# A weight ring of four whole blocks, low parts written over the raw weights, and two row buffers for the gathers of UP, in a decoder block with an expert layer (one core)

## The chip, the core and the metric

The kernel runs on one core of one Trainium2 chip. The metric is the device time of one execution in microseconds; lower is better. The names of the engines in the profile are PE (TensorE), DVE (VectorE), ACT (ScalarE), POOL (GpSimd) and SP (SyncE, which here only issues transfers); PEld is TensorE's weight load.

## What is computed

A decoder block on 256 tokens of width 2048: a mixer (differential attention beside a causal convolution, a shared output projection, norms and gates from a conditioning vector), and then an expert layer, which takes about three quarters of the time and is what the change touches:

```python
q = (h @ w_q).reshape(T, PEER_HEADS, PEER_KEY_DIM)
...
    v1, i1 = lax.top_k(s1, PEER_TOPK)
    v2, i2 = lax.top_k(s2, PEER_TOPK)
...
    top, pos = lax.top_k(cand, PEER_TOPK)
    idx = jnp.take_along_axis(cand_idx, pos, axis=-1)
    g = jax.nn.softmax(top.astype(jnp.float32), axis=-1)
    u = u_tab[idx]
    vv = v_tab[idx]
    act = jax.nn.gelu(jnp.einsum('thkd,td->thk', u, hb).astype(jnp.float32),
                      approximate=False) * g
    return jnp.einsum('thk,thkd->td', act.astype(vv.dtype), vv)
```

There are 16384 experts, each one row of 2048 floats in `u_tab` and one in `v_tab` (128 MB each), and every token picks 16 of them in each of 8 heads.

## The kernel before

**Two ways through the tables.** For 192 of the 256 tokens the kernel computes the products with all experts, and so streams both tables through SBUF in 128 blocks of 1 MB each. For the other 64 tokens it gathers the chosen rows: 64 gathers of 128 rows (1 MB) from `u_rows`, later 64 from `peer_v`, issued by GpSimd (L518).

**Units and phases.** A block is worked on as two units of 128x1024 floats. All weights from the query projection on pass through the same pipeline in five phases: WQ (32 units), UP (64), MID (64), ROUTE (128), all of these with stationary weights from the ring, and DOWN (256 units, the second table). All phases from UP on are loops with 16 units (8 blocks) in one iteration: 4 of UP, 4 of MID, 8 of ROUTE, 16 of DOWN. In the profile WQ runs from 482 us, UP from 586, MID from 745, ROUTE from 934 and DOWN from 1299 to 1964 us.

**What one unit passes through.** SP loads it into one of four places of `raw` (`ring`, 512 KB each). ACT makes its high part, `w_hi` (L720, a rounding copy to the faster matmul format), DVE its low part, `w_lo` = raw - `w_hi` (L379). PE multiplies with `w_hi` (L996 in the products of UP, MID and ROUTE, L1345 in DOWN), then with `w_lo` (L1005, L1345). `w_hi` and `w_lo` have two places each. So ACT's `hi` of unit s waits for its landing, for PE to be through with `w_hi` of unit s-2 (`hi_used`), and for the low part of s-2; the low part of s waits for its high part and for PE to be through with `w_lo` of s-2 (`split_used`); and SP loads unit s when the low part of unit s-4 is made (`slot_free`). `hi_ready`, `lo_ready` and `landed` count what is made and landed.

**What else DVE does between the low parts**, in the order in which the code has it, with no way round for a later instruction: in UP and MID two chains of top-k steps per iteration (`experts`); in MID and ROUTE the dots of gathered rows with the tokens (`dots_at`, L1422, two halves for a row, at the unit numbers in `DOTS_MID`, `DOTS_ROUTE` and their `_FIRST` forms for a phase's first iteration); in ROUTE six sets of masks (`make_masks`, L1387 and L1392); in DOWN half a row per two units added up (`add_row`, L1849) and two groups of gates multiplied and split (L1814, L1821, L1823), whose inputs SP brings back from DRAM (`gel_group`, L423).

**Row buffers.** The rows of `u_rows` land in three buffers (`got[0:3]`), so gather n waits until row n-3 is used (`row_used`). Those of `peer_v` land in four.

**At the end** SP brings back the saved residual (`x_saved`, 2 MB) and ACT, at the start of DOWN, the gate row (`gate_saved`, 1 MB).

## Time and profile before

| | |
|---|---|
| median of 3 runs | 1988.01 us (1985.76 to 1992.11) |
| the profiled execution | 1988.32 us, its span 1986.4 us |
| PE, DVE busy | 92%, 81% |
| ACT, POOL busy | 42%, 8% |
| transfers | 618.02 MB, mean 311 GB/s |

The span is from the first to the last instruction; some 2 us of the execution lie outside it. A share of busy time is an average over stages that differ much, so the stretches of time below are cut at the phases and at whole iterations of their loops. "DMA share" is the mean busy share of the 16 DMA engines.

### The profile page before, as it was taken

The numbers are of one execution on the slowest core, as the hardware profiler recorded it, in microseconds if no ns is written. First come the engines' busy times: TensorE is split into PE (matmuls) and PEld (weight loads), VectorE is DVE, ScalarE is ACT, GpSimd is POOL, SyncE is SP. The second block draws the span as 40 slices with busy tenths as digits, with TensorE's granted clock in tenths as the row PEclk, the third lists the DMA queues.
The fourth block names the chain that finished last, engine by engine and source line by source line (L and its number), as shares of the span: only waits on it lengthen the run. The fifth ranks groups of instructions, "written<-read, shape, count | busy, mean of one in ns | idle before, by whom it ended". The sixth has DMA issues, their size and how long they took to land.

```text
span 1986.4 us, 30520 instructions
## 1 busy us (share of the span) xinstructions
PE 1831.6 (92%) x9902; PEld 1559.0 (78%) x9902; DVE 1611.1 (81%) x2621; ACT 843.9 (42%) x1208; POOL 160.3 (8%) x145
## 2 busy tenths in 40 slices
PE   4999999997999998888899999989999999999997
PEld 4888887435999997778899999976767777777775
DVE  4668898575878999999899999968777777777777
ACT  3011222203545554445455555544444444444444
POOL 0000000000000001000112111111101111011100
PEclk9999999998999999999999999999999999999999
DMA  8997565797886778878899999989998989989895
GB/s 349 417 422 302 218 243 218 320 394 280 302 332 194 235 240 312 284 266 276 302 354 350 357 347 359 350 326 338 320 331 314 337 318 331 330 302 334 321 322 197
DMA packets 135955, 618.02 MB, mean 311 GB/s; under 512 B 16049, under 2 KB 24785, under 8 KB 99025
## 3 DMA queue, kind: packets, MB, share of 16 engines
q1 hardware_dynamic: 105984, 464.57, 63.5%
q0 software_dynamic: 18496, 134.24, 18.9%
q10 hardware_dynamic: 11410, 18.36, 2.5%
q8 instruction: 38, 0.62, 0.1%
q14 instruction: 27, 0.22, 0.0%
HBM read 600.26 MB, written 16.79 MB: 311 GB/s over the span
## 4 chain that ended last, share of the span: by engine, by line
PE 40%; DMA 22%; DVE 20%; issue 12%; ACT 3%; DVEq 1%; SPq 1%; ACTq 0%; POOLq 0%
DMA raw<-in_peer_v 11%; DVE w_lo L379 8%; PE ps L996 6%; PE ps L1043 6%; PE ps L1345 6%; DMA raw<-in_peer_u 5%; PE ps L1204 5%; PE ps L1027 4%; PE ps L1005 4%; PE ps L1154 3%; DVE big L1422 3%; PE ps L1054 3%; DMA early<-in_w_front 2%; ACT w_hi L720 2%; DVE big L1849 2%
## 5 line engine op out<-in xcount | busy, mean ns | idle before, releaser
L720 ACT ACTIVATE w_hi<-raw 128x1024 fp32r<-128x1024 f32 x544 | 577.3, 1063 | 722.1 <-DMA raw<-in_peer_v 151.4
L379 DVE TENSOR_TENSOR w_lo<-raw,w_hi 128x1024 fp32r<-128x1024 f32 x544 | 662.8, 1224 | 206.3 <-ACT w_hi L720 190.1
L1345 PE MATMUL ps<-w_hi,a 128*128 128x512 f32 x1536 | 396.9, 394 | 26.5 <-ACT w_hi L720 19.7
L996 PE MATMUL ps<-a,w_hi 128*128 128x384 f32 x2048 | 412.1, 342 | 6.9 <-ACT stage L822 5.9
L1345 PEld LDWEIGHTS ps<-w_hi,a 128*128 128x128 f32 x1536 | 285.8, 188 | 101.0 <-ACT w_hi L720 34.0
L996 PEld LDWEIGHTS ps<-a,w_hi 128*128 128x128 f32 x2048 | 349.2, 190 | 8.2 <-ACT stage L822 5.6
L1345 PE MATMUL ps<-w_lo,a 128*128 128x512 f32 x1024 | 282.0, 397 | 28.0 <-DVE w_lo L379 27.9
L1005 PE MATMUL ps<-a,w_lo 128*128 128x192 f32 x2048 | 272.1, 275 | 31.0 <-DVE w_lo L379 31.0
L1005 PEld LDWEIGHTS ps<-a,w_lo 128*128 128x128 f32 x2048 | 261.7, 192 | 48.9 <-DVE w_lo L379 48.4
L1345 PEld LDWEIGHTS ps<-w_lo,a 128*128 128x128 f32 x1024 | 187.6, 188 | 90.2 <-DVE w_lo L379 53.5
L1422 DVE CUSTOM_DVE_ANT_0 big<-big 128x1024 f32<-128x1024 f32 x128 | 156.6, 1224 | 2.9 <-DMA big<-in_u_rows,row_ix 2.9
L1447 DVE CUSTOM_DVE_ANT_0 early<-early,big 128x2048 f32<-128x2048 f32 x48 | 109.1, 2289 | 47.9 <-DMA early<-in_w_ada 47.9
L518 POOL DMA_INDIRECT big<-in_u_rows,row_ix x64 | 81.2, 1268 | 811.6 <-DVE dots_now L1422 439.0
L1849 DVE SCALAR_TENSOR_TENSOR big<-big,row_act 128x1024 f32<-128x1024 f32 x94 | 120.3, 1280 | 0.0
L1503 DVE SCALAR_TENSOR_TENSOR big<-big 128x256 f32<-128x256 f32 x240 | 96.5, 483 | 0.0
L1154 PE MATMUL ps<-early,big 128*128 128x512 f32 x192 | 87.5, 610 | 8.3 <-DMA early<-in_w_front 7.6
L1027 PE MATMUL ps<-big,early 128*128 128x256 f32 x384 | 84.4, 380 | 2.5 <-ACT big L594 2.5
L518 POOL DMA_INDIRECT big<-in_peer_v,row_ix x48 | 53.3, 1111 | 409.3 <-DVE big L1849 352.8
L1043 PE MATMUL ps<-big,early 128*128 128x256 f32 x384 | 84.8, 380 | 0.0
L1027 PEld LDWEIGHTS ps<-big,early 128*128 128x128 f32 x384 | 72.5, 190 | 13.8 <-issue 4.2
L1154 PEld LDWEIGHTS ps<-early,big 128*128 128x128 f32 x192 | 36.7, 195 | 56.9 <-issue 44.0
L1043 PEld LDWEIGHTS ps<-big,early 128*128 128x128 f32 x384 | 72.2, 190 | 10.5 <-issue 1.0
(228 smaller groups left out, 1672.6 us busy)
## 6 DMA issues: line engine op xcount, KB each, us to landing
raw<-in_peer_u SPq DMA_DIRECT2D x256, 512.0 KB
raw<-in_peer_v SPq DMA_DIRECT2D x256, 512.0 KB
early<-in_w_ada SPq DMA_DIRECT2D x60, 1024.0 KB, 10.6
early<-in_w_front SPq DMA_DIRECT2D x42, 1024.0 KB, 9.3
raw<-in_w_ada SPq DMA_DIRECT2D x20, 1024.0 KB, 10.7
raw<-in_peer_wq SPq DMA_DIRECT2D x32, 512.0 KB
big<-in_w_gate_f SPq DMA_DIRECT2D x16, 1024.0 KB, 5.2
raw<-in_w_front SPq DMA_DIRECT2D x14, 1024.0 KB, 8.8
```

Source lines behind the costliest of these rows:

```text
L379: engine.tensor_tensor(w_lo[:, s % 2, part], ring[j % ph.ring][:, part], w_hi[:, s % 2, part].bitcast(F32), ALU.subtract)\
L518: gp.indirect_dma_start(where, None, table, bass.IndirectOffsetOnAxis(ap=row_ix[:, n:n + 1], axis=0))\
L720: act.activation(w_hi[:, s % 2, :], ring[j % ph.ring], ACT.Copy).then_inc(hi_ready, 1)
L996: done = pe.matmul(ps[:, b % 2, 0:2 * TD].rearrange("p (m t) -> p m t", m=2), w_hi[:, half, k * P:(k + 1) * P], a_pair[:, kc, :, 0:TD], st ...
L1005: done = pe.matmul(ps[:, b % 2, 0:TD], w_lo[:, half, k * P:(k + 1) * P], a_hi[:, kc, 0:TD], start=False, stop=False, skip_group_check=True)
L1027: done = pe.matmul(ps[:, b // 2, (b % 2) * T:(b % 2 + 1) * T], slots[n % SLOTS][:, b * P:(b + 1) * P], hT[:, k, :], start=k == 0 and b % 2 ...
L1043: done = pe.matmul(ps[:, e % 2, 0:T], slots[n % SLOTS][:, kc * P:(kc + 1) * P], hT[:, kc, :], start=kc == 0, stop=kc == KC - 1)
L1154: done = pe.matmul(ps[:, (MIX_FIRST, MIX_SECOND)[half][bank], :], mixed(place)[:, tt * P:(tt + 1) * P], slots[n % SLOTS][:, cols:cols + 51 ...
L1345: done = pe.matmul(ps[:, 4 * tt + 2 * (j % 2) + n, :], a, w[:, j % 2, n * 512:(n + 1) * 512], start=i is None and blk == 0 and w is w_hi a ...
L1422: d = dve.tensor_tensor_reduce(got[buf][:, cols], got[buf][:, cols], h_tok[:, cols], 1.0, 0.0, ALU.mult, ALU.add, dots_now[:, n, half:half ...
L1447: dve.tensor_tensor_reduce(slots[n % SLOTS], slots[n % SLOTS], c_all, 1.0, 0.0, ALU.mult, ALU.add, macc[:, group, k:k + 1]).then_inc(mod_u ...
L1849: d = dve.scalar_tensor_tensor(acc[:, cols], got[n][:, cols], row_act[:, bass.ds(at(i, 4, n), 1)], acc[:, cols], ALU.mult, ALU.add)
```

## The change

- **The ring** has eight unit places, four pairs (`pairs`). SP loads a whole block, 1 MB, into a pair with one transfer, and ACT waits for it once in two units. A block is loaded when PE is through with the block four before it (`split_used`).
- **The low part** is written to `w_low`, which lies at the same addresses as `raw`: over the raw unit. The two places of `w_lo` are gone, and with them DVE's wait for `split_used`.
- **Row buffers:** two in MID and ROUTE (gather n waits until row n-2 is used), four in DOWN as before. MID's dots are of 4 rows in every iteration (5 in the first and 3 in the others before), ROUTE's of 6 in every iteration (8 in the first and 6 before), at other unit numbers.
- **Loads moved:** the gate row's load goes from ACT at the start of DOWN to SP in DOWN's last iteration, together with the residual's, which was behind the last weight load. The first gates of DOWN are brought back behind the third block instead of the third unit. The 16 loads of 1 MB in WQ (`w_gate_f`) stand later in SP's order (`GATE_AT`).
- `early`, `big` and the regions in them are laid out anew; `Phase` loses its patterns, of which only "w" was in use.

```diff
-GATE_AT = [min(2 * g + 4, g + 18) for g in range(KC)]
+GATE_AT = [7, 7] + [min(2 * g + 8, g + 22) for g in range(2, KC)]
...
-DOTS_MID_FIRST, DOTS_MID = tuple(range(6, 16)), (1, 4, 6, 9, 12, 14)
-DOTS_ROUTE_FIRST, DOTS_ROUTE = tuple(range(16)), (0, 1, 2, 4, 5, 6, 8, 9, 10, 12, 13, 14)
+DOTS_MID_FIRST, DOTS_MID = tuple(range(8, 16)), (1, 2, 5, 6, 9, 10, 13, 14)
+DOTS_ROUTE_FIRST = DOTS_ROUTE = (0, 1, 3, 4, 5, 6, 8, 9, 11, 12, 13, 14)
...
-        raw = sb("raw", [P, RAW, UNIT])
-
-
-        with nc.sbuf_tensor("early", [P, 6 * D], F32) as early:
+        with nc.sbuf_tensor("raw", [P, RING, UNIT], F32) as raw:
+            pass
+        w_low = sb("w_low", [P, RING, UNIT], F32R)
+
+
+        with nc.sbuf_tensor("early", [P, 5 * D], F32) as early:
             pass
...
-        w_lo = sb("w_lo", [P, 2, UNIT], F32R)
...
             def bring(ph, i, w, block0=0, after=None):
...
+                for n in range(ph.blocks):
+                    block = ph.block + n
+                    if block < RING // 2 and i is None:
+                        sp.wait_ge(*consumed(len(LOADS) - SLOTS + block))
                     else:
...
+                        sp.wait_ge(split_used, at(i, ph.per, 2 * block - RING + 2))
+                    src = w[block0 + n] if i is None else \
+                        w[bass.ds(i * ph.blocks + block0 + n, 1)].rearrange("o p n -> (o p) n")
+                    sp.dma_start(pairs[block % 4], src).then_inc(landed[block % 4], 16)
                     if after:
...
-                if j == 2:
+                if j == 5:
                     for half in range(2):
                         sp.wait_ge(gel_out[half], 16)
                     sp.wait_ge(oh_used, TOKEN_GROUPS)
                     gel_group(0, None)
...
+                if j == 7:
+                    sp.wait_ge(at_lo, GROUPS // 2)
+                    sp.dma_start(x_tok.rearrange("p a b -> p (a b)"), x_saved).then_inc(x2_back, 16)
+                    sp.dma_start(gate_f, gate_saved[0, :].partition_broadcast(P)).then_inc(gate_f_back, 16)
...
+            for n in range(ROWS):
+                if n >= 2:
+                    gp.wait_ge(row_used, n - 1)
+                gather(n, u_rows, got[n % 2], row_in[n % 2])
...
-                act.wait_ge(landed[j % ph.ring], ph.landed(j, i))
+                s = ph.s + j
+                if j % 2 == 0:
+                    act.wait_ge(landed[s // 2 % 4], at(i, 16 * ph.blocks // 4, 16 * (s // 8 + 1)))
...
-                if ph.pattern[j] == "w":
-                    low_part(dve, ph, j, i)
+                s = ph.s + j
+                dve.wait_ge(hi_ready, at(i, ph.per, s + 1))
+                dve.tensor_tensor(w_low[:, s % RING, :], raw[:, s % RING, :], w_hi[:, s % 2, :].bitcast(F32),
+                                  ALU.subtract).then_inc(lo_ready, 1)
```

**Where instructions move.** First SP's order at the start of DOWN (`raw` is the ring, `oh` and `stage` are the places of the returned gates). Before:

```order
L402 DMA raw<-in_peer_v 128x1024 [waits lo_ready] x3
L423 DMA oh<-gel_saved 128x768 [waits oh_used,gel_out1,gel_out0]
L402 DMA raw<-in_peer_v 128x1024 [waits lo_ready] x3
L423 DMA stage<-gel_saved 128x768 [waits gel_out1,gel_out0]
L402 DMA raw<-in_peer_v 128x1024 [waits lo_ready] x6
L423 DMA oh<-gel_saved 128x768 [waits at_made]
L402 DMA raw<-in_peer_v 128x1024 [waits lo_ready] x4
```

Now:

```order
L323 DMA raw<-in_peer_v 128x2048 [waits split_used] x3
L342 DMA oh<-gel_saved 128x768 [waits oh_used,gel_out1,gel_out0]
L323 DMA raw<-in_peer_v 128x2048 [waits split_used]
L342 DMA stage<-gel_saved 128x768 [waits gel_out1,gel_out0]
L323 DMA raw<-in_peer_v 128x2048 [waits split_used] x2
L342 DMA oh<-gel_saved 128x768 [waits at_made]
L323 DMA raw<-in_peer_v 128x2048 [waits split_used] x2
```

Each weight load is of 128x2048 where it was of 128x1024, waits for `split_used` in place of `lo_ready`, and the first gates stand behind three whole blocks.

Second, GpSimd's gathers, of which the rows with `in_u_rows` are those of MID and ROUTE. Before:

```order
L518 DMA big<-in_u_rows,row_ix 128x2048 [waits row_ix_in,gate_f_saved]
L518 DMA big<-in_u_rows,row_ix 128x2048 x2
L518 DMA big<-in_u_rows,row_ix 128x2048 [waits row_used] x61
L518 DMA big<-in_peer_v,row_ix 128x2048 [waits row_used] x3
L518 DMA early<-in_peer_v,row_ix 128x2048 [waits split_used]
L518 DMA big<-in_peer_v,row_ix 128x2048 [waits v_row_used] x3
```

Now:

```order
L439 DMA big<-in_u_rows,row_ix 128x2048 [waits row_ix_in,gate_f_saved]
L439 DMA big<-in_u_rows,row_ix 128x2048
L439 DMA big<-in_u_rows,row_ix 128x2048 [waits row_used] x62
L439 DMA big<-in_peer_v,row_ix 128x2048 [waits row_used] x2
L439 DMA early<-in_peer_v,row_ix 128x2048 [waits split_used] x2
L439 DMA big<-in_peer_v,row_ix 128x2048 [waits v_row_used] x2
```

Two gathers go out without waiting for a used row, where there were three. The second and third rows of `peer_v` now wait for the end of the products, since two of the four buffers lie in `early`.

Third, DVE in the first iteration of ROUTE, from its third unit on (L1422, now L1314, are the dots; L379, now L1292, the low parts; `row_in` counts landed gathers). Before:

```order
L379 TENSOR_TENSOR w_lo<-raw,w_hi 128x1024 [waits split_used,hi_ready]
L1422 ISA big,dots_now<-big 128x1024 [waits row_in0]
L1422 ISA dots_now 128x1
L379 TENSOR_TENSOR w_lo<-raw,w_hi 128x1024 [waits split_used,hi_ready]
L1422 ISA big,dots_now<-big 128x1024
L1422 ISA dots_now 128x1
L1802 COPY sel_T<-ps 128x384 [waits selT_ready]
L1803 COPY sel_T<-ps 128x192
L1387 TENSOR_TENSOR oh<-iota,sel_T 128x512 [waits vec]
L1392 TENSOR_SCALAR oh<-iota,sel_T 128x128 x4
L379 TENSOR_TENSOR w_lo<-raw,w_hi 128x1024 [waits split_used,hi_ready]
L1422 ISA big,dots_now<-big 128x1024 [waits row_in1]
```

Now:

```order
L1292 TENSOR_TENSOR w_low<-raw,w_hi 128x1024 [waits hi_ready] x2
L1314 ISA big,dots_now<-big 128x1024 [waits row_in1]
L1314 ISA dots_now 128x1
L1694 COPY sel_T<-ps 128x384 [waits selT_ready]
L1695 COPY sel_T<-ps 128x192
L1277 TENSOR_TENSOR oh<-iota,sel_T 128x512 [waits vec]
L1282 TENSOR_SCALAR oh<-iota,sel_T 128x128 x4
L1292 TENSOR_TENSOR w_low<-raw,w_hi 128x1024 [waits hi_ready]
L1314 ISA big,dots_now<-big 128x1024
L1314 ISA dots_now 128x1
L1292 TENSOR_TENSOR w_low<-raw,w_hi 128x1024 [waits hi_ready]
L1314 ISA big,dots_now<-big 128x1024 [waits row_in0]
```

The third unit has no dot any more, and the row that was second begins one unit later; over the iteration 12 halves stand where 16 stood.

## Rows read from the trace of the kernel before

**Rows 1.** Busy time by stretch: PE, PEld, DVE, ACT, POOL, clock, DMA share, GB/s.
```profile
50.00:100.00 50.00, 50.00 (x233) 44.03 (x232) 30.56 (x41) 4.22 (x7) 0.00 (x0) 1.00 1.01 418
...
586.60:745.00 158.40, 157.41 (x1086) 153.27 (x1086) 141.91 (x402) 89.97 (x140) 0.00 (x0) 1.00 0.71 229
745.00:795.00 50.00, 41.72 (x268) 38.97 (x266) 45.30 (x120) 21.29 (x32) 7.80 (x7) 0.97 0.89 312
795.00:934.40 139.40, 121.06 (x795) 111.56 (x794) 128.46 (x342) 64.14 (x96) 9.86 (x9) 1.00 0.81 275
934.40:992.60 58.20, 50.25 (x334) 48.01 (x333) 51.80 (x90) 29.70 (x41) 8.83 (x8) 0.94 0.86 298
992.60:1299.40 306.80, 302.54 (x2173) 299.61 (x2172) 295.77 (x500) 181.30 (x268) 58.02 (x43) 1.00 0.96 353
1299.40:1346.60 47.20, 39.60 (x176) 32.16 (x176) 31.02 (x35) 20.37 (x24) 5.71 (x5) 0.93 0.89 327
1346.60:1925.40 578.80, 533.67 (x2239) 412.46 (x2238) 449.52 (x422) 258.08 (x252) 61.74 (x56) 1.00 0.90 325
1925.40:1963.50 38.10, 35.27 (x152) 27.88 (x151) 30.43 (x30) 16.61 (x17) 1.14 (x1) 1.00 0.80 272
```

**Rows 2.** Waits in DOWN, 1346.6 to 1925.4 us: total, times, longest.
```profile
ACT w_hi L720 <- DMA raw<-in_peer_v: 137.9, 88, 5.1
DVE w_lo L379 <- ACT w_hi L720: 129.3, 110, 4.7
ACT w_hi L720 <- PE ps L1345: 78.3, 59, 4.1
...
PE ps L1345 <- DVE w_lo L379: 26.5, 54, 0.7
PE ps L1345 <- ACT w_hi L720: 18.1, 23, 1.7
```

**Rows 3.** Timeline, TensorE in DOWN: start, duration, idle before.
```profile
1619.47 1.53 PE L1345 MATMUL ps<-w_hi,a 128*128 128x512 f32 x6
...
1621.74 1.52 PE L1345 MATMUL ps<-w_hi,a 128*128 128x512 f32 x6
...
1626.81 1.65 PE L1345 MATMUL ps<-w_hi,a 128*128 128x512 f32 x6 [0.37 <-ACT w_hi L720]
```

**Rows 4.** VectorE's groups by line in ROUTE's loop, 992.6 to 1299.4 us.
```profile
L379 DVE TENSOR_TENSOR w_lo<-raw,w_hi 128x1024 fp32r<-128x1024 f32 x112 | 136.7, 1226 | 8.4 <-ACT w_hi L720 8.0
L1422 DVE CUSTOM_DVE_ANT_0 big<-big 128x1024 f32<-128x1024 f32 x85 | 104.1, 1224 | 0.0
L1392 DVE TENSOR_SCALAR oh<-iota,sel_T 128x128 f32<-128x128 f32 x168 | 46.8, 353 | 0.0
L1387 DVE TENSOR_TENSOR oh<-iota,sel_T 128x512 f32<-128x512 f32 x42 | 29.0, 690 | 1.6 <-PE ps L1298 1.3
```

**Rows 5.** Line 518's gathers in the same stretch.
```profile
  DVE dots_now L1422: 253.3, 43
...
DMA to landing us min/median/max: 8.0/8.8/9.5
```

**Rows 6.** Timeline in ROUTE: end of one row's dots, and the next gather.
```profile
1204.30 0.10 DVE L1422 DVE_READ_ACCUMULATOR2_ANT dots_now<- 128x1 f32 x1
...
1204.67 0.94 POOL L518 DMA_INDIRECT big<-in_u_rows,row_ix  x1 [5.65 <-DVE dots_now L1422]
```

**Rows 7.** Waits, 745 to 795 us: the only wait of a dot for its row.
```profile
DVE big L1422 <- DMA big<-in_u_rows,row_ix: 2.9, 1, 2.9
```

**Rows 8.** Timeline, the start of DOWN.
```profile
1298.01 0.54 SPq L423 DMA_DIRECT2D oh<-gel_saved  x1
...
1307.27 0.96 DVE L1814 TENSOR_TENSOR big<-big,oh 128x768 f32<-128x768 f32 x1 [2.53 <-DMA oh<-gel_saved]
...
1310.27 2.04 PE L1345 MATMUL ps<-w_hi,a 128*128 128x512 f32 x4 [6.33 <-DVE a L1823]
```

**Rows 9.** The DMA queue's own waits over the whole span.
```profile
SPq L402 <- DVE w_lo L379: 1092.0, 499, 22.0
```

More of the change, by code:

```diff
@@ L27 @@
 LOWEST = -3e38
-RAW = 4
-WIDE = 8
+RING = 8
 UNIT = 1024
```

237 lines of the change are left out of this document (68 added, 169 removed).

## The prediction

> **What bounds the kernel now.** I read first the busy time by stretch [rows 1], cut at the phases, then the waits of the longest stretch, then single instructions.
>
> In [rows 1] the reader is to see four regimes. From 586.6 to 745 us (UP) PE is busy 157.41 of 158.40 us at a DMA share of 0.71: PE is the bound. From 795 to 934.4 (three iterations of MID, 46.5 us each) PE has 121 of 139.4 us and DVE 128.5: DVE, whose dots stand between the top-k chains, is the bound. From 992.6 to 1299.4 (seven iterations of ROUTE, 43.8 us each) PE has 302.5 of 306.8, DVE 295.8, and the DMA share is 0.96: all three are full, so nothing is to be won there and any new wait of DVE costs its length. From 1346.6 to 1925.4 (fourteen iterations of DOWN, 41.34 us each) PE has 533.7 of 578.8, DVE only 449.5, and the DMA share is 0.90.
>
> In that last stretch ACT waits 137.9 us for loads and DVE 129.3 us for ACT [rows 2]; PE waits 26.5 us for low and 18.1 us for high parts. The waits put down to PE (78.3 us) can hide late loads too, since a wait for several things is named by one. [Rows 3] shows what a unit takes when all is there: 2.27 us from one start to the next (1619.47, 1621.74). Sixteen are 36.3 us. So each iteration loses 5.0 us, 70 us in the stretch; the 44.6 us in which PE is shown idle are the lower reading of the same loss, since a matmul whose end is modelled covers short gaps. SP waited 1092 us for low parts [rows 9]: the transfers start as soon as a place is free, and the places are too few.
>
> **The change, part by part.**
>
> *Ring in DOWN.* Before, unit s+4 is loaded when the low part of s is made, at best 1.3 us after PE begins s-1, and its high part is due 1.5 us after PE begins s+2: three units and 0.2 us, 7.0 us. Now a block is loaded when PE ends the one four before it, and due when PE has 0.7 us left of the fifth unit after: 10.6 us. The load has twice the bytes; at the rate of 50 to 100 us, where all loads are of 1 MB (418 GB/s at a share of 1.01, so 414 [rows 1]), 512 KB more are 1.3 us. So 2.3 us more room remain; a gather (1 MB, 2.5 us) and two group loads in an iteration no longer empty the ring. ACT's, DVE's and PE's own work is as before. DVE's missing wait for `split_used` is worth nothing: the high part of the same unit waits for nearly the same point (`hi_used` of s-2).
>
> How fast can it then go? An iteration moves 325 GB/s x 41.34 us = 13.4 MB, 8.4 of them weights. At 414 GB/s for the weights, and for the rest at DOWN's present 325/0.90 = 361, the DMA engines need 20.3 + 13.9 = 34.2 us. With PE at 36.3 that is a share of 0.94; ROUTE runs at 0.96 with PE full. The ends: PE's 36.3 us; and 38.8 us if the larger loads bring no rate (13.4 MB at 361 x 0.96). I take 37.2, nearer PE's end because ROUTE shows PE full at such a share. 41.34 - 37.2 = 4.1, times 14: **-58** (ends -70 and -36).
>
> The Trainium skill (DMA: Bandwidth & Descriptors, "Specifications") speaks against more: it gives HBM some 358 GB/s for each core. By it an iteration takes 13.4/0.358 = 37.5 us and the stretch wins 54 instead of 58 us, 1942 us in all. The 418 GB/s of [rows 1] do not agree with it, so it is not used.
>
> *First and last iteration of DOWN.* At the start PE stands 6.33 us for the low part of the gates, which come from a load issued at 1298.01 and used at 1307.27 [rows 8]. That load now stands behind a load of 1 MB in place of 512 KB: +1.3; the other 38 us of the iteration gain 1, and the gate row's 1 MB is away: 0. The last (38.10 us, share 0.80, hardly a gather) now carries 3 MB of residual and gate row in front of four weight loads, 7.6 us of DMA time, of which the ring covers most: +1 (0 to +4). It hides behind PE; with the ring empty it would cost all 7.6.
>
> *Two row buffers in ROUTE.* Now gather n waits until row n-2 is used. In the loop's order the next row of the same buffer is due four units later for four rows of six, five for two. Between lie, on DVE, 4 low parts, 2 halves of dots and 2 mask sets: 4 x 1.23 + 2 x (1.22 + 0.10) + 2 x (0.69 + 4 x 0.28) = 11.2 us [rows 4, 6] (0.28 is 46.8 over 168). The same sum over a whole iteration gives 46.4, but 43.8 are there, since neighbours overlap: x 0.94, so 10.6 us of room. Needed: 0.27 from the dots' end to the gather [rows 6], 8.8 to landing (at most 9.5, [rows 5]), 0.1: 9.2, at most 9.9. It fits by 1.4 us today. Now the gather finds up to 512 KB more of weights in front: up to +1.3, so that the slower ones come up to 0.6 us late. With 32 such rows in eight iterations, half of them late by 0.3: **+5** (0 to +20).
>
> The Trainium skill (same page, "Queues, rings and completion order") says that an engine drains a whole packet of descriptors from one queue before it turns to the next. A weight load's packet would then be twice as long, which is the same 1.3 us; no row shows this, and it changes no term.
>
> *Dots moved.* A half costs DVE 1.3 us. The three later iterations of MID get two more: DVE is the bound, +7.8. The first has two fewer, -2.6, and the one wait for a row (2.9 us [rows 7]) may go, since the first dot stands two units later: -1.4 taken. ROUTE's first has four fewer, -5.2 if DVE bounds it; its 58.2 us hold 51.8 of DVE and 50.3 of PE [rows 1], so half, -2.6. **+1** (-4 to +5). In MID the next row of a buffer is due seven units later, 20 us: no wait.
>
> *WQ.* The gates' loads of 1 MB stand up to four units later and behind 1 MB; DVE may stand for them, with PE two units of cover: **+1** (0 to +5). *UP:* 0, PE is full. *Front:* same loads and slots: 0.
>
> Sum: -58 + 0 + 1 + 5 + 1 + 1 = -50. The profiled execution took 1988.3 us (the median of the runs is 1988.0, the same), so **1938 us**.
>
> **The rivals.**
>
> *A. DMA becomes DOWN's bound.* The engines are at 0.90 now, and the larger loads bring no rate: 38.8 us an iteration, -36 instead of -58: **1960**. For it: ROUTE never exceeds 353 GB/s in seven iterations. Against: ROUTE is held by PE and DVE, and 418 GB/s were moved with 1 MB loads.
>
> *B. The gathers in ROUTE become the bound: slower.* Today a gather of 1 MB has the engines almost to itself, 2.5 us of the 8.8. If it must share them evenly with a weight queue that is never empty, its data take 5.1 us, and with 0.6 in front it lands after 12.0, needed 12.4 against 10.6: 1.8 late at four rows and, with one unit (2.7 us) more, at none of the others. 7.2 x 8 iterations = +58 in place of +5: with DOWN's gain still there **1991**. It decides from 1.7 us of lateness on (55 us over 32 rows); below, the sum stays faster. For it: DVE has no reserve there. Against: a median of 8.8 and a maximum of only 9.5 at a share of 0.96.
>
> *C. The change doesn't do what it says in DOWN.* The loads arrive early, but DVE's order (half rows, groups) and the two places of `w_hi` hold PE back as now. PE's waits for low parts (26.5 us) are the larger ones. Against: DVE's own waits of 129.3 us are for ACT, and its work is 32.1 of 41.3 us. A gain of 17 in DOWN, 9 in all: **1979**.
>
> **How the numbers follow.** Forecast (1920 to 1950) 0.62; A (to 1970) 0.20; C (to 1982) 0.08; B, whole or nearly, 0.10, of which 0.03 end within 0.3%, which is 6 us and about what a measurement of this kernel can tell from no change. So faster 0.90, same 0.03, slower 0.07. The low end is DOWN at PE's pace and nothing lost in ROUTE: 1988 - 70 + 3 = 1921. Range 1920 to 1970, which leaves out C and B, 0.18.
>
> **What would show it.** DOWN's iterations at 37.2 us with a DMA share over 0.9, ACT's wait for `in_peer_v` under 40 us there, PE's idle time under 20. ROUTE's iterations at 44.0 to 44.7 with some waits of the dots for `in_u_rows`, MID's later ones at 49. The prediction is wrong if these waits in ROUTE exceed 20 us, if DOWN stays above 39 us with DMA full (A) or with DVE's low parts late (C), or if another stretch moves by over 5 us.

## The result, and the profile after

The changed kernel takes 1896.93 us (median of 4 runs, 1893.89 to 1903.56) against 1986.88 us (1981.47 to 1992.11) of the kernel before on the same chip: a ratio of 0.9552 (95% interval 0.9514 to 0.959), 90 us less. The forecast was 1938 us, its range 1920 to 1970: the sign was right, the gain nearly twice as large, the time outside the range. The profiled execution took 1894.76 us, its span 1892.9 us, against 1986.4 before.

Busy time by stretch of the changed kernel, with the columns of [rows 1] (the first two give the stretch and its length in us), cut at the same events: UP, the first and the three later iterations of MID, the first and the seven later ones of ROUTE, the first, the fourteen middle ones and the last of DOWN.

```profile
583.20:745.60 162.40, 160.68 (x1121) 157.39 (x1119) 148.92 (x409) 92.43 (x144) 0.00 (x0) 1.00 0.68 237
745.60:788.40 42.80, 38.66 (x265) 36.96 (x263) 41.41 (x114) 20.96 (x33) 4.83 (x5) 1.00 0.86 323
788.40:930.80 142.40, 121.28 (x793) 110.86 (x793) 134.78 (x354) 65.01 (x97) 13.31 (x12) 1.00 0.80 288
930.80:985.10 54.30, 48.59 (x334) 47.17 (x335) 49.07 (x86) 29.79 (x42) 10.31 (x7) 0.97 0.81 301
985.10:1284.50 299.40, 299.31 (x2173) 299.15 (x2172) 293.24 (x496) 186.90 (x268) 57.68 (x43) 1.00 0.93 359
1284.50:1327.70 43.20, 38.79 (x173) 32.27 (x172) 31.06 (x35) 20.38 (x24) 6.71 (x6) 0.92 0.91 347
1327.70:1835.90 508.20, 508.20 (x2242) 420.23 (x2241) 447.87 (x423) 258.77 (x253) 80.10 (x57) 1.00 0.97 371
1835.90:1870.00 34.10, 34.10 (x152) 28.06 (x151) 29.42 (x29) 16.60 (x17) 1.06 (x1) 1.00 0.76 310
```

Three things are to be read against [rows 1]. DOWN's middle stretch is 508.2 us long instead of 578.8, and PE is busy in all of it. ROUTE's loop, which PE seemed to fill already (302.5 of 306.8 us), is 299.4 us long, 7.4 less, for the same 2173 matmul records. And both move more than before: 359 GB/s in ROUTE, at a share of 0.93 where it was 0.96 for 353, and 371 in DOWN, at 0.97 where it was 0.90 for 325.

The waits in DOWN's middle stretch, in the form of [rows 2]: ACT's 137.9 us for loads are gone, no wait for a transfer is left on a compute engine, and what ACT waits for is PE.

```profile
ACT w_hi L616 <- PE ps L1235: 217.0, 197, 1.4
...
DVE w_low L1292 <- ACT w_hi L616: 60.3, 83, 1.0
ACT a L810 <- DVE big L1706: 33.6, 28, 1.2
...
PEld ps L1235 <- DVE w_low L1292: 0.7, 3, 0.3
```

The start of three units on TensorE there, against [rows 3]: 2.26 and 2.27 us from one to the next. The fourteen iterations take 36.27 to 36.65 us each, sixteen such units.

```profile
1618.94 1.52 PE L1235 MATMUL ps<-w_hi,a 128*128 128x512 f32 x6
...
1621.20 1.52 PE L1235 MATMUL ps<-w_hi,a 128*128 128x512 f32 x6
...
1623.47 1.52 PE L1235 MATMUL ps<-w_hi,a 128*128 128x512 f32 x6
```

The start of DOWN, against [rows 8]: the first gates' load is issued at 1283.09, used at 1289.38, and PE stands 3.83 us instead of 6.33.

```profile
1283.09 0.33 SPq L342 DMA_DIRECT2D oh<-gel_saved  x1
...
1289.38 0.95 DVE L1706 TENSOR_TENSOR big<-big,oh 128x768 f32<-128x768 f32 x1
...
1292.42 1.19 PE L1235 MATMUL ps<-w_hi,a 128*128 128x512 f32 x2 [3.83 <-DVE a L1715]
```

The DMA queue's own waits, against [rows 9]: SP now waits for PE's ends of units (L894 in the products, L1235 in DOWN).

```profile
SPq L323 <- PE ps L894: 625.6, 128, 11.1
SPq L323 <- PE ps L1235: 466.6, 124, 4.2
```

Lines of the page: PE is busy 95% (92% before), and the chain that ended last is 73% PE (40% before; the last line is that of the kernel before).

```profile
PE 1796.9 (95%) x9902; PEld 1564.3 (83%) x9902; DVE 1605.2 (85%) x2621; ACT 850.1 (45%) x1208; POOL 181.2 (10%) x145
...
DMA packets 96785, 617.98 MB, mean 326 GB/s; under 512 B 11697, under 2 KB 20433, under 8 KB 25041
...
PE 73%; DVE 13%; issue 7%; DMA 6%; ACT 1%; DVEq 0%; ACTq 0%; SPq 0%
```

```profile
PE 40%; DMA 22%; DVE 20%; issue 12%; ACT 3%; DVEq 1%; SPq 1%; ACTq 0%; POOLq 0%
```

Where the 93.5 us of the span went, from the start of the high part (on ACT) of each stage's first unit to that of the next (us; "each" is the mean of the iterations behind the first, in DOWN of the fourteen middle ones; "last" is counted to the start of the last unit's high part, fifteen units):

| | WQ | UP 1st, each | MID 1st, each | ROUTE 1st, each | DOWN 1st, each, last | in all |
|---|---|---|---|---|---|---|
| before | 119.1 | 48.3, 38.31 | 49.7, 46.47 | 58.2, 43.82 | 47.2, 41.35, 38.1 | |
| after | 118.9 | 49.7, 37.56 | 42.8, 47.47 | 54.3, 42.77 | 43.2, 36.30, 34.1 | |
| change | -0.3 | -0.8 in all | -3.9 in all | -11.3 in all | -78.6 in all (-4.0, -70.7, -4.0) | -94.9 |

The front, ahead of WQ, is 1.4 us longer (463.0 to 464.4), the close is the same 22.9 us.

These times come from one profiled execution of each kernel. Among the kernels below that have the same code in a stage, the later iterations agree within 0.1 us in most cases, but the first ones don't: UP's take 48.2 to 49.7 us, ROUTE's 54.3 to 56.2, DOWN's 42.9 to 49.2. So the changes of -3.9 us in ROUTE's and -4.0 in DOWN's first iteration are uncertain by some us.

### The profile page after: what moved, and what is told of

Its sections match the earlier page's. It is cut to its first block, busy times and chain, and to the rows that moved or that the text cites. A ratio compares the mean times of both kernels' runs of the same rounds, so it can differ in the third digit from the quotient of the medians.

```text
span 1892.9 us, 29014 instructions
## 1 busy us (share of the span) xinstructions
PE 1796.9 (95%) x9902; PEld 1564.3 (83%) x9902; DVE 1605.2 (85%) x2621; ACT 850.1 (45%) x1208; POOL 181.2 (10%) x145
## 3 DMA queue, kind: packets, MB, share of 16 engines
q1 hardware_dynamic: 66960, 465.60, 64.1%
## 4 chain that ended last, share of the span: by engine, by line
PE 73%; DVE 13%; issue 7%; DMA 6%; ACT 1%; DVEq 0%; ACTq 0%; SPq 0%
PE ps L1235 31%; PE ps L887 10%; PE ps L894 6%; PE ps L932 6%; PE ps L916 4%; PE ps L1093 4%; PE ps L1043 3%; PE ps L943 3%; DMA early<-in_w_front 2%; DVE w_low L1292 2%; PE ps L1187 2%; DVE big L1314 2%; DMA early<-in_w_ada 1%; DMA big<-in_w_gate_f 1%; DMA gsub<-in_g_subln 1%
## 5 line engine op out<-in xcount | busy, mean ns | idle before, releaser
L1292 DVE TENSOR_TENSOR w_low<-raw,w_hi 128x1024 fp32r<-128x1024 f32 x544 | 661.5, 1221 | 103.2 <-ACT w_hi L616 95.1
L1235 PE MATMUL ps<-w_hi,a 128*128 128x512 f32 x1536 | 391.2, 390 | 3.8 <-DVE a L1715 3.8
L887 PEld LDWEIGHTS ps<-a,w_hi 128*128 128x128 f32 x2048 | 347.6, 189 | 5.9 <-ACT stage L716 4.1
L1235 PEld LDWEIGHTS ps<-w_hi,a 128*128 128x128 f32 x1536 | 288.9, 188 | 64.3 <-issue 4.0
L894 PEld LDWEIGHTS ps<-a,w_low 128*128 128x128 f32 x2048 | 261.7, 191 | 41.6 <-DVE w_low L1292 40.4
L894 PE MATMUL ps<-a,w_low 128*128 128x192 f32 x2048 | 270.2, 274 | 27.3 <-DVE w_low L1292 27.1
L1235 PE MATMUL ps<-w_low,a 128*128 128x512 f32 x1024 | 274.6, 390 | 0.0
L1235 PEld LDWEIGHTS ps<-w_low,a 128*128 128x128 f32 x1024 | 192.5, 188 | 40.7 <-DVE w_low L1292 0.7
L1314 DVE CUSTOM_DVE_ANT_0 big<-big 128x1024 f32<-128x1024 f32 x128 | 155.7, 1217 | 0.0
L1339 DVE CUSTOM_DVE_ANT_0 raw<-raw,big 128x2048 f32<-128x2048 f32 x32 | 73.0, 2288 | 27.6 <-DMA raw<-in_w_ada 27.6
L1741 DVE SCALAR_TENSOR_TENSOR big<-early,row_act,big 128x1024 f32<-128x1024 f32 x64 | 81.8, 1278 | 0.0
L1093 PE MATMUL ps<-a,w_hi 128*128 128x256 f32 x512 | 69.4, 290 | 0.9 <-DVE a L1569 0.9
L439 POOL DMA_INDIRECT big<-in_peer_v,row_ix x32 | 44.4, 1389 | 250.1 <-DVE big L1741 206.7
L439 POOL DMA_INDIRECT early<-in_peer_v,row_ix x32 | 44.8, 1399 | 226.0 <-DVE big L1741 222.8
L1093 PEld LDWEIGHTS ps<-a,w_hi 128*128 128x128 f32 x512 | 65.0, 196 | 1.2 <-DVE a L1569 1.2
## 6 DMA issues: line engine op xcount, KB each, us to landing
early<-in_w_ada SPq DMA_DIRECT2D x40, 1024.0 KB, 10.3
```

The source lines that it names most:

```text
L439: gp.indirect_dma_start(where, None, table, bass.IndirectOffsetOnAxis(ap=row_ix[:, n:n + 1], axis=0))\
L887: done = pe.matmul(ps[:, b % 2, 0:2 * TD].rearrange("p (m t) -> p m t", m=2), w_hi[:, half, k * P:(k + 1) * P], a_pair[:, kc, :, 0:TD], st ...
L894: done = pe.matmul(ps[:, b % 2, 0:TD], w_low[:, s % RING, k * P:(k + 1) * P], a_hi[:, kc, 0:TD], start=False, stop=False, skip_group_check ...
L1093: return pe.matmul(ps[:, banks[blk // 2], (blk % 2) * T:(blk % 2 + 1) * T], w[:, blk * P:(blk + 1) * P], a[:, k, :], start=k == 0 and m == ...
L1235: done = pe.matmul(ps[:, 4 * tt + 2 * (j % 2) + n, :], a, w[:, n * 512:(n + 1) * 512], start=i is None and blk == 0 and m in (0, 2), stop= ...
L1292: dve.tensor_tensor(w_low[:, s % RING, :], raw[:, s % RING, :], w_hi[:, s % 2, :].bitcast(F32), ALU.subtract).then_inc(lo_ready, 1)
```

## The experiments

All have the same stages, so one table serves them (us, read as above; the time is the median of all runs of each, the ratio is to the kernel before on the same chip, with its 95% interval).

| kernel | time | ratio | WQ | UP 1st, each | MID 1st, each | ROUTE 1st, each | DOWN 1st, each, last |
|---|---|---|---|---|---|---|---|
| e1_units_deep | 1895.67 | 0.9535 (0.9515-0.9554) | 119.1 | 48.2, 37.56 | 42.8, 47.50 | 56.2, 42.85 | 46.2, 36.30, 34.0 |
| e2_units_four | 2076.44 | 1.044 (1.0419-1.0461) | 179.8 | 63.5, 37.59 | 45.2, 47.49 | 57.7, 43.61 | 59.8, 41.62, 39.6 |
| e3_blocks_three | 2016.60 | 1.0147 (1.013-1.0164) | 188.6 | 58.4, 37.56 | 45.4, 47.49 | 55.9, 43.39 | 57.6, 37.74, 37.2 |
| e4_low_waits | 1905.26 | 0.9596 (0.9576-0.9617) | 119.2 | 48.8, 38.32 | 44.2, 48.39 | 55.1, 42.77 | 43.5, 36.30, 34.7 |
| e5_four_old_order | 1983.57 | 0.999 (0.9971-1.0009) | 119.2 | 48.2, 37.56 | 45.3, 47.37 | 55.1, 44.50 | 45.9, 41.29, 41.1 |
| e6_old_order | 1894.58 | 0.9544 (0.9525-0.9562) | 117.3 | 48.2, 37.56 | 42.8, 47.48 | 55.5, 42.77 | 43.3, 36.30, 34.1 |
| e7_units_room_six | 2036.65 | 1.0266 (1.0234-1.0297) | 182.9 | 60.6, 37.56 | 44.5, 47.48 | 55.4, 44.66 | 46.4, 39.65, 40.7 |
| e8_saved_last | 1896.10 | 0.9556 (0.9539-0.9573) | 118.7 | 49.1, 37.56 | 42.8, 47.47 | 55.1, 42.77 | 45.8, 36.30, 34.0 |
| e9_gathers_late_a | 1912.72 | 0.9617 (0.9585-0.965) | 118.7 | 48.9, 37.51 | 43.0, 47.50 | 52.5, 45.19 | 47.9, 36.30, 34.9 |
| e10_gathers_late_b | 1924.53 | 0.969 (0.9656-0.9725) | 118.5 | 49.3, 37.51 | 43.0, 47.50 | 52.7, 46.55 | 42.9, 36.30, 34.4 |
| e11_pool_lows | 1893.28 | 0.9524 (0.9497-0.9552) | 118.9 | 49.2, 37.56 | 44.4, 45.80 | 55.1, 42.93 | 49.2, 36.30, 34.0 |
| e12_units_room_eight | 1927.03 | 0.9688 (0.9656-0.9721) | 135.5 | 53.1, 37.56 | 42.9, 47.50 | 55.8, 42.83 | 43.3, 37.02, 35.2 |

### The size of the transfers, and the depth of the ring

**e1_units_deep**: eight places as in the changed kernel, but filled 512 KB at a time, each when PE is through with the unit eight before.

```diff
-                        sp.wait_ge(split_used, at(i, ph.per, 2 * block - RING + 2))
...
-                    sp.dma_start(pairs[block % 4], src).then_inc(landed[block % 4], 16)
+                        sp.wait_ge(split_used, at(i, ph.per, s - RING + 1))
...
+                    sp.dma_start(raw[:, s % RING, :], src).then_inc(landed[s % RING], 16)
```

> The changed kernel, but each weight load is again of 512 KB (one unit), into the same ring of eight places, each place loaded when PE is through with its unit. The room between a load's issue and its use is 6 units less 0.7 us, 12.9 us (2.27 us a unit in DOWN), the largest of all. Theory R (the room was what the kernel before lacked): DOWN's loop at PE's pace, 36.3 to 36.6 us an iteration, the whole within 0.3% of the changed kernel (1895 to 1901 us). Theory S (the size of a transfer is what brings the rate): DOWN's iterations at 38.5 us or more, ROUTE's at 43.8, the whole 1930 us or more. For the gathers in ROUTE (7.3 to 7.8 us to landing in the changed kernel, 8.8 before): if 8 KB pieces in the weight queue speed them up, they are back at 8.8 or more here; if it is the room, they stay under 8.

The same time as the changed kernel, and DOWN's iterations are the same 36.30 us. So the 1 MB transfers are not what won. The windows row of its DOWN loop has even the same rate:

```profile
1329.50:1837.60 508.10, 508.10 (x2241) 420.32 (x2240) 447.84 (x423) 258.65 (x252) 80.13 (x57) 1.00 0.98 371
```

What the size does change is the gathers beside the loads: in ROUTE's loop the mean from issue to landing is 9.5 us here and 7.7 us in the changed kernel. Ten dots wait for their rows here, 3.9 us in all (at most 0.9), and none in the changed kernel; the loop is only 0.08 us an iteration longer.

**e2_units_four**: the kernel of e1, but unit s is loaded when the low part of unit s-4 is made, which is the release of before; all else of the change stays (shown against e1).

```diff
-                        sp.wait_ge(split_used, at(i, ph.per, s - RING + 1))
+                        sp.wait_ge(lo_ready, at(i, ph.per, s - 3))
...
```

> As the kernel with 512 KB loads in the ring of eight places, but a unit is loaded only when the low part of the unit four before is made: the rule and the size of the kernel before (room 7.0 us), with the low parts in place, two row buffers and the moved loads of the change. Theory R: DOWN's iterations back at 41.3 us, ROUTE's at 43.8, the whole at 1970 to 1985 us. Theory L (the low parts written in place, without a wait for PE, are what brought the gain): DOWN's iterations under 37.5 us and the whole under 1920 us. With two row buffers and the old traffic ROUTE's gathers are back at 8.8 us to landing, and some dots may wait for their rows.

DOWN falls back to 41.62 us an iteration: the depth is the gain there. But 1.044 is far more than the gain undone: WQ takes 179.8 us instead of 118.9, UP's and DOWN's first iterations lose 14 and 17. The total lies 91 us above what Theory R expected, a surprise that the next kernel had to settle.

**e5_four_old_order**: e2, with the loads that the change moved back at their old places in SP's order.

```diff
-GATE_AT = [7, 7] + [min(2 * g + 8, g + 22) for g in range(2, KC)]
+GATE_AT = [min(2 * g + 4, g + 18) for g in range(KC)]
...
-                if j == 5:
+                if j == 2:
...
-                if j == 7:
+                if j == 5:
```

> The kernel with unit loads of 512 KB released by the low part of unit s-4, and in addition the gate loads of WQ and the first returned gates of DOWN at the places in SP's order that they had before the change. Theory K (the moved loads need the deep ring: at their new places they hold a shallow ring back): the 80 us lost in WQ, the 14 in UP's first and the 13 in DOWN's first iteration come back, DOWN's loop stays at 41 to 42.5 us an iteration, in all 1972 to 1985 us, a few us under the kernel before, because the low part no longer waits. Theory L (the low parts over the raw units or the two row buffers cost that time in a shallow ring): it stays at 2060 to 2080 us.

Theory K holds: 0.999 (0.9971 to 1.0009), which can't be told from the kernel before. VectorE's waits for the gates' loads from 463 to 645 us show the mechanism; first e2, then e5, then the changed kernel (total, times, longest):

```profile
DVE big L1333 <- DMA big<-in_w_gate_f: 79.4, 12, 8.6
```

```profile
DVE big L1333 <- DMA big<-in_w_gate_f: 0.4, 1, 0.4
```

```profile
DVE big L1332 <- DMA big<-in_w_gate_f: 20.5, 13, 4.4
```

In e2's timeline at the start of WQ one sees it for a unit. Two gate loads go out at 492.82 only, behind weight loads that SP may issue only when DVE's low parts (L1293) are made; DVE then stands for the first of them (L1333, 2.87 us), and with it its next low parts, and so SP's next loads.

```profile
492.82 0.90 SPq L386 DMA_DIRECT2D big<-in_w_gate_f  x2
...
494.46 1.23 DVE L1293 TENSOR_TENSOR w_low<-raw,w_hi 128x1024 fp32r<-128x1024 f32 x1 [1.51 <-ACT w_hi L617]
...
495.71 0.33 SPq L326 DMA_DIRECT2D raw<-in_peer_wq  x1
...
498.55 1.29 DVE L1333 SCALAR_TENSOR_TENSOR big<-big,cT 128x1024 f32<-128x1024 f32 x1 [2.87 <-DMA big<-in_w_gate_f]
```

Not all of WQ's 61 us are waits. For the same work, some 675 matmul records, PE needs 140 us from 500 us on in e2 and 80 us in e5 (the first row is e2's):

```profile
500.00:640.00 140.00, 98.73 (x676) 96.53 (x675) 63.43 (x62) 40.79 (x57) 0.00 (x0) 0.83 0.50 178
```

```profile
500.00:580.00 80.00, 80.00 (x674) 80.00 (x673) 63.87 (x60) 39.76 (x57) 0.00 (x0) 1.00 0.89 328
```

PE stands idle for 41 of these 60 us. The other 19 are its own work, which takes longer, since the granted clock was 0.83 there: it fell from 2.4 to 1.2 GHz nine times, for 3.4 or 6.8 us each, every time at a stand of PE of 2.4 to 7.0 us.

So e5 tells two things at once: all other parts of the change together (low parts in place, two row buffers, moved dots; 512 KB loads) are worth nothing in a ring of four, and the loads may stand at their new places only because the ring is deep. What is won beside it (UP 2.3, MID 1.7, ROUTE's first iteration 3.0 us) goes back in ROUTE's loop, 4.7 us (44.50 us an iteration against 43.82), and in DOWN. Its waits there name the place, ACT for weights and, five times, the dots for a row:

```profile
ACT w_hi L617 <- DMA raw<-in_peer_u: 94.2, 45, 4.7
...
DVE big L1315 <- DMA big<-in_u_rows,row_ix: 4.4, 5, 1.3
```

**e3_blocks_three**: 1 MB at a time, a block loaded when PE is through with the block three before, so that 6.1 us remain until its first high part is due (by the count of the prediction; 10.6 in the changed kernel).

```diff
-                        sp.wait_ge(split_used, at(i, ph.per, 2 * block - RING + 2))
+                        sp.wait_ge(split_used, at(i, ph.per, 2 * block - RING + 4))
```

> The changed kernel, but a block is loaded only when PE is through with the block three before it in place of four: 1 MB loads with 10.6 - 4.5 = 6.1 us of room. Theory R: a load of 1 MB takes 2.5 us on the engines beside a gather of 2.5, so 6.1 us are less than the kernel before had with half the bytes: DOWN's iterations at 42 to 45 us, the whole at 1990 to 2030 us. Theory S: the rate comes from the size, so DOWN stays under 38.5 us and the whole under 1935 us.

Both theories miss. DOWN's iterations take 37.74 us, where R had 42 to 45, and the whole 2016.60 us, where S had under 1935: WQ takes 188.6 us, and VectorE waits 80.8 us there for the gates' loads, as in e2.

**e7_units_room_six** and **e12_units_room_eight**: 512 KB at a time, released by PE's end of unit s-5 and of s-6, 6.1 and 8.4 us ahead (the gates of DOWN at their old place, as in e5). The line of e7 is shown against e1; that of e12 has `+ 3` for `+ 4`.

```diff
-                        sp.wait_ge(split_used, at(i, ph.per, s - RING + 1))
+                        sp.wait_ge(split_used, at(i, ph.per, s - RING + 4))
```

> 512 KB loads of a unit each into the eight places, but unit s is only loaded when PE is through with unit s-5, so that 6.1 us remain until its high part is due, as in the kernel that loads whole blocks with three blocks of ring (the first returned gates of DOWN stand at their old place, since at the new one this ring would never fill). Theory R (the room alone sets DOWN's pace): DOWN's loop as there, 37.8 to 38.5 us an iteration, ROUTE's 42 to 44. Theory S (the larger transfers help where the room is short): 39.5 to 42 us an iteration. WQ and the first iterations will lose much here as there; the total, 1990 to 2080 us, decides nothing.

> 512 KB loads, unit s loaded when PE is through with unit s-6 (8.4 us until its high part is due, one unit more than in the kernel with 6.1 us, one less than with 10.6), first returned gates of DOWN at their old place. Theory R (the loss falls with the room and is gone where the slowest load, 9 to 12 us after its issue, no longer comes late): DOWN's loop 36.6 to 37.8 us an iteration, between 39.6 at 6.1 us and 36.3 at 12.9. Rival T (a threshold: all or nothing): 36.3 already here, and WQ without loss. The total, 1895 to 1960 us, hangs on WQ too.

The DOWN loops of e3, e7 and e12, fourteen iterations each, as windows rows:

```profile
1431.90:1960.30 528.40, 516.49 (x2240) 417.40 (x2239) 448.01 (x422) 255.66 (x252) 82.28 (x57) 1.00 0.93 356
```

```profile
1418.70:1973.70 555.00, 529.52 (x2240) 414.13 (x2240) 449.13 (x422) 258.64 (x252) 70.53 (x57) 1.00 0.92 339
```

```profile
1348.40:1866.70 518.30, 514.11 (x2244) 418.99 (x2243) 449.10 (x424) 257.47 (x253) 80.77 (x57) 1.00 0.98 364
```

With e5 and e1 this is a curve. Measured for the 224 units of the loop (112 blocks), from the issue of a load to the start of the high part of its first unit, and then the iteration:

| kernel | a load waits for | least time | mean | an iteration |
|---|---|---|---|---|
| before | low part of s-4 | 4.8 us | 7.1 us | 41.35 us |
| e5 | low part of s-4 | 4.8 | 7.0 | 41.29 |
| e7 | PE's end of s-5 | 5.8 | 7.3 | 39.65 |
| e3 | PE's end, three blocks | 5.8 | 6.8 | 37.74 |
| e12 | PE's end of s-6 | 8.0 | 8.5 | 37.02 |
| changed | PE's end, four blocks | 10.3 | 10.5 | 36.30 |
| e1 | PE's end of s-8 | 12.5 | 12.7 | 36.30 |

So the loss falls by degrees as the room grows, and is gone at four blocks: of the 3.35 us an iteration that e7 loses against the changed kernel, e12 loses 0.72, within what Theory R gave for it. Rival T fails with it. But between e3 and e7, whose loops differ in the size of the loads alone, Theory R fails and S holds: 37.74 and 39.65 us at the same release and the same least time. Where the room is short, whole blocks do better. The reason was not separated: a block's second unit is due one unit (2.27 us) later than its first, so half of e3's units have 8.4 us; and gathers land sooner beside whole blocks (in DOWN after 7.6 us in the mean in e3, 9.3 in e7). The release by the low part is the worst, at nearly the same mean: its least time is 4.8 us, where the prediction counted 7.0. No kernel has the low part's release with more room, or PE's with as little, so what the releasing engine does by itself was not separated from the room.

### The low part's missing wait

**e4_low_waits**: the changed kernel, with the wait that low parts over the raw unit don't need.

```diff
                 dve.wait_ge(hi_ready, at(i, ph.per, s + 1))
+                if s >= 2 or i is not None:
+                    dve.wait_ge(split_used, at(i, ph.per, s - 1))
                 dve.tensor_tensor(w_low[:, s % RING, :], raw[:, s % RING, :], w_hi[:, s % 2, :].bitcast(F32),
```

> The changed kernel, but DVE's low part of unit s waits again until PE is through with the low part of s-2. Theory R and S, and the prediction (the missing wait is worth nothing): within 0.3% of the changed kernel, 1895 to 1901 us. Theory L: DVE may no longer run ahead, DOWN's iterations rise by 0.5 us or more, and the whole by 8 us or more.

1905.26 us, a ratio of 0.9596 (0.9576 to 0.9617); beside e1 (0.9515 to 0.9554) on the same chip the loss is clear, by span it is 7.4 us. It lies where DVE has much besides low parts: UP's later iterations take 38.32 us again, as before the change (38.31), MID's 48.39 instead of 47.47, and its first 44.2 instead of 42.8. ROUTE's loop and DOWN's don't move, so Theory L, which expected the loss in DOWN, has its size and not its place. The three later iterations of UP in e4, 114.9 us where they are 112.7 in the changed kernel (114.9 before the change too):

```profile
632.20:747.10 114.90, 114.24 (x793) 112.12 (x792) 104.92 (x300) 63.15 (x96) 0.00 (x0) 1.00 0.71 240
```

In UP TensorE's weight loads wait eight times for a low part, 3.0 us in all, in e4 as before the change, and four times, 1.3 us, in the changed kernel. By the order of the code a wait at the head of a low part holds back the top-k chain behind it on DVE's queue, and so the next low parts; that chain of causes was not followed in the trace. The prediction called the wait worth nothing.

### The loads moved, in a deep ring

**e6_old_order**: the changed kernel with the edit of e5 (without its ring). **e8_saved_last**: the residual and the gate row behind the last weight load.

```diff
-                if j == 7:
+                if j == 15:
                     sp.wait_ge(at_lo, GROUPS // 2)
                     sp.dma_start(x_tok.rearrange("p a b -> p (a b)"), x_saved).then_inc(x2_back, 16)
```

> The changed kernel with the gate loads of WQ and the first returned gates of DOWN back at their old places in SP's order (counted in units; a block is two). Theory K: with four whole blocks in the ring the places hardly matter, 1893 to 1902 us, WQ 119 us in all as now, DOWN's first iteration 43 to 45 us. Rival M: the new places are worth something of their own; the old ones stall the weight loads behind waits for used gates and cost 5 to 20 us in WQ, 1902 to 1917 us in all.

> The changed kernel with the loads of the residual and the gate row (3 MB) behind the last weight load instead of in front of the last four. Theory K: DOWN's last iteration takes 34 us as now, since the room of the ring covers 3 MB in front of four blocks; the rows come 3 to 8 us later, and what the closing stretch waits for them is lost: 1897 to 1905 us. Rival N: the 4 us that the last iteration won come partly from this place; then the total goes the other way or the last iteration changes by over 1 us.

Neither place matters: 1894.58 and 1896.10 us. In e6 WQ takes 117.3 us, DOWN's first iteration 43.3, so Rival M fails. In e8 DOWN's last iteration takes 34.0 us as with the 3 MB in front, and the close is no longer. Theory K's loss in the close didn't come, and the total lies just under its range. So the 4.0 us won in the last iteration are the ring's, which covers 3 MB without loss in either order; in the ring of four the same iteration takes 41.1 us (e5).

### Two row buffers: how much time is to spare

**e9_gathers_late_a**, **e10_gathers_late_b**: GpSimd clears a tile of its own ten or twenty times before each of ROUTE's 48 gathers.

```diff
                 if n >= 2:
                     gp.wait_ge(row_used, n - 1)
+                if n >= ROW_ROUTE_FIRST:
+                    for k in range(10):
+                        gp.memset(idle[:, :], 0.0).then_inc(idled, 1)
+                        gp.wait_ge(idled, 10 * (n - ROW_ROUTE_FIRST) + k + 1)
                 gather(n, u_rows, got[n % 2], row_in[n % 2])
```

> The changed kernel, in which GpSimd clears a small tile of its own ten times before each of ROUTE's 48 gathers, an estimated 2 to 2.5 us (a clear of 128x128 takes 0.20 us in the trace of the changed kernel, and the semaphore behind each adds to it). Theory G (two buffers leave 10.0 to 11.5 us of room, the gathers land after 7.7 us in the mean, 10.1 at most, so about 2.5 us are to spare): about half of the rows come late by up to 2 us, 10 to 30 us in all, 1907 to 1927 us. Theory H (the stall is absorbed, since PE has two units of work ahead when DVE waits): at most 1905 us.

> As the kernel with ten clears, with twenty: 4 to 5 us. Theory G: nearly every row comes late, by 1.5 to 2.5 us in the mean, and each costs its lateness: 60 to 110 us in ROUTE, 1955 to 2005 us in all. Theory H: at most 1930 us.

The delay in e9 and the waits of the dots for their rows from 1030 to 1290 us, then the same wait in e10, whose twenty clears take 3.6 us:

```profile
1200.00 1.96 POOL L452 MEMSET idle<- 128x16 f32 x10 [4.47 <-DVE dots_now L1320]
1202.23 2.43 POOL L441 DMA_INDIRECT big<-in_u_rows,row_ix  x1 [0.27 <-POOL idle L452]
```

```profile
DVE big L1320 <- DMA big<-in_u_rows,row_ix: 20.8, 11, 2.1
```

```profile
DVE big L1320 <- DMA big<-in_u_rows,row_ix: 24.9, 17, 2.7
```

In e9, 2.0 us of delay cost 2.4 us an iteration (nothing in the first of the loop, 3.0 in the others) and 13 to 16 us in all: Theory G. In e10, 3.6 us cost 3.8 us an iteration and 27 us in all, less than half of what G expected and within what H allowed, but not for H's reason: DVE waits 24.9 us in that stretch, and the 5.6 iterations in it lose 21, so hardly anything is absorbed. G's rows were less late than it took them to be. With the delay a gather goes out 3.95 us after the dots and lands 7.5 us later; 0.1 us on, 11.6 us are needed, 1.0 more than the 10.6 of the prediction, which at four rows of six makes 4 us an iteration by the prediction's own count. A second thing may lower the price of a late row. A stall of DVE before row n lies within the room of two gathers, row n's and that of row n+1, which is in flight at the same time: the next one finds its room longer by the stall (in e10 the rooms were 10.7 to 13.1 us, 10.0 to 11.5 in the changed kernel). One stall then serves two rows. Neither account was tested by a run of its own.

### MID, which VectorE bounds

**e11_pool_lows**: GpSimd makes the low parts of units 4 and 12 of each iteration of MID.

```diff
                 gather(n, u_rows, got[n % 2], row_in[n % 2])
+                if n in LOW_AFTER:
+                    unit = LOW_AFTER.index(n)
+                    s = PH_MID.s + 16 * (unit // 2) + (4, 12)[unit % 2]
+                    gp.wait_ge(hi_ready, s + 1)
+                    gp.wait_ge(lo_ready, s)
+                    gp.tensor_tensor(w_low[:, s % RING, :], raw[:, s % RING, :], w_hi[:, s % 2, :].bitcast(F32),
+                                     ALU.subtract).then_inc(lo_ready, 1)
...
```

> The changed kernel, in which GpSimd makes two of the sixteen low parts of each iteration of MID (units 4 and 12) in place of VectorE. Theory V (DVE's work bounds MID: 134.8 of 142.4 us, PE 121.3): each of the three later iterations loses up to 2 x 1.22 us, 45.0 to 45.8 us instead of 47.2, 1889 to 1893 us in all. Theory X (GpSimd takes several times as long for it, or slows DVE's own instructions beside it): MID as now or up to 8 us longer, 1896 to 1905 us.

MID's later iterations take 45.80 us instead of 47.47, as Theory V has it. A low part takes 2.43 us on GpSimd, and 1.22 us on DVE, beside it as well (group row; busy, mean ns, idle and releaser). The second row is the window of the three later iterations:

```profile
L455 POOL TENSOR_TENSOR w_low<-raw,w_hi 128x1024 fp32r<-128x1024 f32 x8 | 19.4, 2429 | 6.8 <-DVE w_low L1303 6.7
```

```profile
789.70:927.10 137.40, 123.81 (x794) 112.84 (x794) 127.76 (x348) 65.50 (x97) 28.04 (x18) 0.99 0.81 297
```

In all it took 1893.28 us, 0.9524 (0.9497 to 0.9552), at the upper end of what V gave. That is the least of all kernels here, but it can't be told apart from the changed kernel (0.9514 to 0.959), e1 or e6. In its profiled execution the 5 us won in MID's loop go again in DOWN's first iteration (49.2 us), because PE there stands until the first gates are back from DRAM; the chain that ended last has their load as one piece:

```profile
1281.17 12.52 DMA oh<-gel_saved
```

That stall is 3.8 us in the changed kernel's profile and 9.6 here, and it is the one place where kernels with the same code there differ by several us (42.9 to 49.2 us for the iteration). What decides how late that one load lands was not tried.

## Why the prediction was wrong

**Ring in DOWN, -58: right mechanism, undersized; -70.7.** The step that failed is "How fast can it then go?". The share after was put at 0.94 and a loss of 0.9 us an iteration kept, for want of a row that shows PE full at it. Measured are a share of 0.97, 371 GB/s and not one lost us: 36.30 us, the lower end that the prediction had named. e1 shows the same with 512 KB, so the steps on the rate of larger transfers (414 GB/s for the weights) had no part in it: the room did it. The "room" before was counted at its best case, 7.0 us; the least was 4.8, since the release hung on DVE's low part, which half rows and groups push back. The Trainium skill (DMA: Bandwidth & Descriptors, "Specifications") gives some 358 GB/s for a core, as half of what a stack of HBM gives its two cores; here one core runs, and the 371 GB/s over 508 us are above the figure, so it was right not to go by it.

**First and last iteration of DOWN, 0 and +1: -4.0 and -4.0.** The last was a wrong sign: the 3 MB in front of four loads cost nothing (e8), and the deep ring takes from this iteration what it takes from the others. It moved 272 GB/s at a share of 0.80 before [rows 1], which was read as no shortage, but ACT waited three times for a load there too, 6.0 us in all and up to 4.8. Of the first one's -4.0, 2.5 us are the shorter stand of PE (6.33 to 3.83), which is 3.6 to 9.6 us in the kernels with the same code there, so it can't be called the ring's; 1.5 us are left for the rest of the iteration.

**Two row buffers in ROUTE, +5: the mechanism exists, but not here.** No dot waits for a row in the changed kernel:

```profile
POOL big L439 <- DVE dots_now L1314: 246.2, 43, 6.8
ACT w_hi L616 <- PE ps L887: 101.5, 76, 2.0
...
DVE oh L1277 <- PE ps L1187: 5.0, 13, 0.6
```

The room was 10.0 to 11.5 us (10.6 predicted), but the gathers became faster, 7.7 us in the mean where they took 9.2, and not up to 1.3 us slower. The 8.8 us (at most 9.5) that the sum used were misread: that line of [rows 5] rests on two gathers at 1293 and 1299 us, the first rows for DOWN, and the forty of ROUTE's loop took 7.3 to 11.0 us. By 9.2 in the mean the fit would have been 1.0 us and not 1.4. With the queue of 512 KB loads (e1, e5) they take 9.5 and 9.4, and there the waits for rows exist, 3.9 and 4.4 us. The Trainium skill (same page, "Queues, rings and completion order") says that an engine drains a whole packet of one queue before it turns to the next; the prediction took from it that larger pieces in the weight queue delay a gather. The pieces did become larger (66960 packets in that queue of the profile where there were 105984), and the gathers landed sooner.

**"All three are full, so nothing is to be won there": ROUTE's loop won 7.4 us.** This reading of [rows 1] is the second step that failed. Busy 302.5 of 306.8 us is no proof of full pace, since the profile models the end of a matmul and the modelled end can cover a wait. The waits of the same stretch before the change, which the prediction left out, show it:

```profile
ACT w_hi L720 <- DMA raw<-in_peer_u: 75.8, 37, 4.6
```

That the ring took them away is shown by e5 and e6, which differ in the ring and its loads alone: 44.50 and 42.77 us an iteration. The test that would have served was the one used in DOWN, the start-to-start time of a unit; the iterations scattered from 43.0 to 44.5 us before, and are 42.99 us each, to the hundredth, in five of seven now (the first is 41.44, the last 43.04).

**Dots moved, +1: -7.8** (MID -3.9 where +3.8 stood, ROUTE's first iteration -3.9 where -2.6 stood). MID's later iterations became 1.0 us longer each, not 2.6: 0.9 of the difference is the missing wait's by e4 (48.39 to 47.47). Its first became 6.9 us shorter, not 4.0: by e4 the wait is 1.4 of it (44.2 to 42.8) and by e5 the deep ring 2.5 (45.3 to 42.8), which leaves 3.0 for the dots if the parts add up.

**DVE's missing wait, nothing: about 7** (UP's later iterations 2.3, MID 4.1, ROUTE's first 0.8, by e4). The argument that it is worth nothing is the third step that failed. It was that `hi_used` of s-2 comes at nearly the same point. But that wait stands on ACT, which has little else to do, and this one on DVE, with a chain of top-k steps behind it.

**WQ +1, UP 0:** -0.3 and -0.8. UP was called full as ROUTE was, and its later iterations still won 0.75 us each, by the missing wait; its first is 1.4 us longer, within the spread of that iteration. And e2 shows what WQ's moved loads would have cost in a shallow ring: 61 us. The prediction took the parts one at a time and so did not see that one protects the other.

The rivals: A (DMA bound) fails by 371 GB/s, C by the 36.30 us an iteration. B's condition isn't met, since the gathers land sooner and not later. Its way of pricing a late row comes out near in e10: 11.6 us needed there make 4 us an iteration, and 3.8 were measured. B's own 12.4 us were not reached by any kernel.

The 43.5 us between -50 and the -93.5 of the span are then DOWN 21.6, ROUTE's loop 12.4 (+5 to -7.4), the dots with the missing wait in them 9, WQ and UP 2, less 1.4 in front, to within the rounding.
